# Loads of the state space issued by ScalarE, weight sums made beside the sparse attention's projections, another order in the last feed-forward

## The reference, cut to what matters

```python
att = dsa_attention(q_lat, c_kv, q_idx, k_idx, w_idx, rel_bias)   # top 128 keys by an index score
y   = ssd_scan(xh, dt, a, bm, cm)                                 # 4 groups x 4 chunks of 128 tokens
x   = x + (sigmoid(g_att) * y_att + sigmoid(g_ssm) * y_ssm) @ w_out
u   = causal_depthwise_conv(rmsnorm(x) @ w_ffn_up, conv_w, conv_b)   # 3 taps, 2 x 2816 channels
gate, val = split(u)
x   = x + (silu(gate) * val) @ w_ffn_down
```

## Time and profile before

| | |
|---|---|
| median of 3 runs | 2824.82 us (2823.62 to 2826.15) |
| the profiled execution | 2823.57 us, of which span 2821.8 us |
| TensorE matmuls busy | 95% of the span |
| VectorE, ScalarE, GpSimd busy | 60%, 46%, 7% |
| mean granted TensorE clock | 0.987 |
| HBM read, written | 439.29 MB, 159.51 MB |

### The profile page before, as it was taken

How to read it: one execution, slowest core, us unless ns; L and a number is a source line. 1 busy time by engine, 2 the same in 40 slices (tenths; PEclk the granted TensorE clock), 3 DMA queues, 4 the chain that set the end, 5 groups by cost and what they waited for, 6 DMA issues and landing times.

```text
span 2821.8 us, 43044 instructions
## 1 busy us (share of the span) xinstructions
PE 2683.9 (95%) x16783; PEld 2283.3 (81%) x16783; DVE 1681.2 (60%) x2880; ACT 1285.4 (46%) x2071; POOL 199.6 (7%) x253
## 2 busy tenths in 40 slices
PE   7999999999999999999999999889977999999997
PEld 6877889999889789689898777657756777798996
DVE  3444486264655455585374428763767975686774
ACT  3456455153535335364262534443443453465551
POOL 1110100001000000000000010330111110000000
PEclk9999999999999999999999999999998999999999
DMA  9984836858475464837352234203699792254441
GB/s 352 205 194 102 202 90 226 207 172 247 109 220 167 132 172 143 237 101 207 108 183 93 74 109 155 78 31 130 206 234 222 216 206 105 82 165 150 149 165 52
DMA packets 173724, 451.52 MB, mean 160 GB/s; under 512 B 15064, under 2 KB 15064, under 8 KB 172896
## 3 DMA queue, kind: packets, MB, share of 16 engines
q1 hardware_dynamic: 108656, 265.34, 27.7%
q0 software_dynamic: 62432, 176.17, 26.7%
q10 hardware_dynamic: 2448, 7.41, 0.7%
HBM read 439.29 MB, written 159.51 MB: 212 GB/s over the span
## 4 chain that ended last, share of the span: by engine, by line
PE 76%; DVE 9%; ACT 5%; issue 5%; DMA 4%; POOL 0%; ACTq 0%; DVEq 0%; POOLq 0%
PE ps L405 26%; PE ps L1505 22%; PE ps L554 5%; PE ps L3248 4%; PE ps L2285 2%; PE ps L1942 2%; DMA weight_sums<-in_weights 2%; PE ps L912 2%; DVE w_lo L376 2%; DMA steps_abc<-acum_rows 2%; PE ps L2087 2%; PE ps L1969 2%; PE ps L791 2%; PE ps L2814 1%; ACT w_hi L368 1%
## 5 line engine op out<-in xcount | busy, mean ns | idle before, releaser
L376 DVE TENSOR_TENSOR w_lo<-raw,w_hi 128x1024 fp32r<-128x1024 f32 x502 | 613.7, 1223 | 502.5 <-ACT w_hi L368 501.6
L368 ACT ACTIVATE w_hi<-raw 128x1024 fp32r<-128x1024 f32 x502 | 528.1, 1054 | 508.5 <-PE ps L405 301.3
L1505 PE MATMUL ps<-x_hi,w_hi 128*128 128x264 f32 (+1 forms) x1120 | 319.4, 285 | 9.6 <-DVE f_in L3398 7.8
L1505 PE MATMUL ps<-x_hi,w_lo 128*128 128x264 f32 (+1 forms) x1120 | 317.6, 284 | 0.0
L1505 PE MATMUL ps<-x_lo,w_hi 128*128 128x264 f32 (+1 forms) x1120 | 317.3, 283 | 0.0
L405 PE MATMUL ps<-x_hi,w_hi 128*128 128x512 f32 (+1 forms) x704 | 257.4, 382 | 36.4 <-DVE w_lo L376 17.3
L405 PE MATMUL ps<-x_lo,w_hi 128*128 128x512 f32 (+1 forms) x704 | 253.1, 376 | 0.0
L405 PE MATMUL ps<-x_hi,w_lo 128*128 128x512 f32 (+1 forms) x704 | 251.8, 375 | 0.0
L1505 PEld LDWEIGHTS ps<-x_hi,w_hi 128*128 128x128 f32 x1120 | 212.1, 189 | 15.6 <-DVE f_in L3398 7.5
L1505 PEld LDWEIGHTS ps<-x_lo,w_hi 128*128 128x128 f32 x1120 | 212.3, 190 | 0.5
L1505 PEld LDWEIGHTS ps<-x_hi,w_lo 128*128 128x128 f32 x1120 | 212.6, 190 | 0.0
(11 more groups left out here) (489 smaller groups left out, 5926.9 us busy)
## 6 DMA issues: line engine op xcount, KB each, us to landing
raw<-in_weights SPq DMA_DIRECT2D x257, 512.0 KB
raw<-weight_sums SPq DMA_DIRECT2D x280, 256.0 KB
weight_sums<-in_weights POOLq DMA_DIRECT2D x36, 1536.0 KB, 19.4
raw<-in_weights SPq DMA_DIRECT2D x210, 256.0 KB
weight_sums<-in_weights POOLq DMA_DIRECT2D x12, 2048.0 KB, 31.2
weight_sums<-in_weights POOLq DMA_DIRECT2D x12, 1792.0 KB, 18.9
weight_sums<-weight_sums POOLq DMA_DIRECT2D x12, 1536.0 KB, 14.3
weight_sums<-weight_sums POOLq DMA_DIRECT2D x4, 2048.0 KB, 20.3
```

The source lines that it names most:

```text
L368: nc.scalar.activation(w_hi[:, s], raw[:, s], ACT.Copy).then_inc(hi_ready, 1)
L376: nc.vector.tensor_tensor(w_lo[:, s], raw[:, s], w_hi[:, s], ALU.subtract).then_inc(lo_ready, 1)
L1505: last = nc.tensor.matmul(out_, w[:, s, 4 * (b % 2) + k], a, start=kind in "125" and k == n == 0, stop=k == 3 and n == 2, skip_group_check ...
```

## The change

It has three parts. The loads of `steps_abc` go from GpSimd to ScalarE: loads 0 and 1 after the second item of the first inputs, load n + 1 when chunk n begins. The first two groups of weight sums go into `dsa_loads`, behind the first four bias loads and ahead of the wait for `selected`; the copies of the third go to the end of `dsa_loads`, its three sums to `ssm_loads`. In the feed-forward the gate inputs have three buffers in place of two (`x_sum` is the third), the convolutions and what follows are put at later blocks (for the last two tiles at earlier ones), ScalarE splits the next chunk ahead of the pieces where no down chunk is at that block, and the down chunk at block 130 goes behind the last block.

```diff
-MIXED = {"sevenf": (54, 58, 64, 68, 74, 78, 84, 90, 98, 104, 110, 116, 122, 130, 140, 142)}
+MIXED = {"sevenf": (54, 58, 64, 68, 74, 78, 84, 90, 98, 104, 110, 116, 122, 140, 142, 144)}
...
             for h in range(4):
                 near_load(h)
+            for group in (FFN_SUMS, FFN_SUMS + 1):
+                for part in SUM_PARTS:
+                    part(pool, group)
             pool.wait_ge(selected, 1)
...
             pool.dma_start(gate[:].rearrange("p k n -> p (k n)"), gate_dram).then_inc(gate_in, 16)
+            sums_copy(pool, FFN_SUMS + 2)
...
+        def steps_load(eng, n):
+            g, c = divmod(n, CH)
+            src = bass.AP(tensor=acum_dram.tensor, offset=8 * g * SEQ + c * P, ap=[[0, P], [SEQ, 8], [1, P]])
+            eng.dma_start(steps_abc[:, n % 2], src).then_inc(abc_in[n % 2], 16)
...
             pool.wait_ge(acum_out, 16)
-            for n in range(SSM_GROUPS * CH):
-                g, c = divmod(n, CH)
-                if n >= 2:
-                    pool.wait_ge(abc_used, n - 1)
-                src = bass.AP(tensor=acum_dram.tensor, offset=8 * g * SEQ + c * P, ap=[[0, P], [SEQ, 8], [1, P]])
-                pool.dma_start(steps_abc[:, n % 2], src).then_inc(abc_in[n % 2], 16)
-                for step in ((2 * n, 2 * n + 1) if n < 6 else (n + 6,)):
-                    if step < len(SUM_STEPS):
-                        sums_step(pool, step)
-                if c == 2 and g in (1, 2):
+            for part in SUM_PARTS[1:]:
+                part(pool, FFN_SUMS + 2)
+            for g in range(1, SSM_GROUPS):
+                if g < SSM_GROUPS - 1:
                     pool.wait_ge(u_norm, 4 * g)
                     kept_back(pool, z_buf, 4 * (g - 1), z_in)
-                if c == 2 and g == SSM_GROUPS - 1:
+                else:
                     pool.wait_ge(u_lo_s, 4 * g)
                     kept_back(pool, gates, 8, gates_in)
...
-            for item in FIRST_ITEMS[0:6]:
+            for i, item in enumerate(FIRST_ITEMS[0:6]):
                 item_split(act, item, split_hi)
                 item_act(act, item)
+                if i == 1:
+                    act.wait_ge(acum_out, 16)
+                    for n in range(2):
+                        steps_load(act, n)
...
                     act.wait_ge(dec_args, n + 1)
+                    if 1 <= n < SSM_GROUPS * CH - 1:
+                        act.wait_ge(abc_used, n)
+                        steps_load(act, n + 1)
...
+                self.gate_in = [self.f_in[:, 0], self.f_in[:, 2], x_sum[:, 0:SEQ + 4]]
...
-                    at_ = dict(tap_v=b4 + 1, conv_v=b4 + 2, tap_g=b3 + 1, conv_g=b3 + 2, silu=b3 + 4, prod=b3 + 5, hi=b3 + 6, lo=b3 + 7)
+                    at_ = dict(tap_v=b4 + 1, conv_v=b4 + 3, tap_g=b3 + 2, conv_g=b3 + 4, silu=b3 + 6, prod=b3 + 7, hi=b3 + 8, lo=b3 + 9)
                     if i == SEVEN["sevenf"] - 2:
-                        at_.update(silu=b3 + 3, prod=b3 + 4, hi=b3 + 4, lo=b3 + 5)
+                        at_.update(conv_v=b4 + 2, tap_g=b3 + 1, conv_g=b3 + 2, silu=b3 + 3, prod=b3 + 3, hi=b3 + 4, lo=b3 + 4)
                     if i == SEVEN["sevenf"] - 1:
-                        at_.update(tap_v=b3 + 2, tap_g=b3 + 2, conv_v=b3 + 3, conv_g=b3 + 3, silu=b3 + 4, prod=b3 + 4, hi=b3 + 5, lo=b3 + 5)
+                        at_.update(tap_v=b3 + 1, tap_g=b3 + 1, conv_v=b3 + 2, conv_g=b3 + 2, silu=b3 + 3, prod=b3 + 3, hi=b3 + 4, lo=b3 + 4)
...
+            def inputs_free(self, eng, f, half):
+
+                wait(eng, f_conved, 2 * (f - 2) + 1 if half else 2 * (f - 3) + 2)
...
                     for c in mixed_at(name, b):
                         split_hi(act, Step(mixed_chunk(name, c) + AHEAD))
+                    behind = mixed_at(name, b)
+                    if not behind and b % 2 == 0 and b < len(order):
+                        split_hi(act, Step(seven_chunk(name, b) + AHEAD))
                     for piece, f in self.steps.get(b, ()):
...
-                    if b % 2 == 0 and b < len(order):
+                    if behind and b < len(order):
                         split_hi(act, Step(seven_chunk(name, b) + AHEAD))
```

More of the change, by code:

```diff
@@ L348, in program @@
         FFN_SUMS = len(SUM_GROUPS) - 3
[L349 to L357, removed]
         SUM_PARTS = (sums_copy, sums_of_two, sums_of_three, sums_of_four)
@@ L3191, in slot, with inputs @@
                 return 2 * (f % 2) + half
+            def inputs(self, f, half):
+                return self.f_in[:, self.slot(f, 1)] if half else self.gate_in[f % 3]
             def part(self, i, half, tokens):
-                return self.f_in[:, self.slot(i + 2, half), 2 + self.w * tokens:2 + self.w * (tokens + 1)]
+                return self.inputs(i + 2, half)[:, 2 + self.w * tokens:2 + self.w * (tokens + 1)]
+            def inputs_free(self, eng, f, half):
+                wait(eng, f_conved, 2 * (f - 2) + 1 if half else 2 * (f - 3) + 2)
             def taps(self, f, half):
@@ L3206, in tap @@
                 slot = self.slot(f, half)
-                nc.scalar.activation(self.f_conv[:, slot], self.f_in[:, slot, 2:2 + SEQ], ACT.Identity,
+                nc.scalar.activation(self.f_conv[:, slot], self.inputs(f, half)[:, 2:2 + SEQ], ACT.Identity,
                                      scale=par[:, w(2)], bias=par[:, b]).then_inc(f_begun, 1)
@@ L3224, in conv @@
                 slot = self.slot(f, half)
-                convolve(dve, self.f_conv[:, slot], 3, w, self.f_in[:, slot], b, f_conved, begun=True)
+                convolve(dve, self.f_conv[:, slot], 3, w, self.inputs(f, half), b, f_conved, begun=True)
             def product(self, dve, f):
@@ L3240, in pool @@
                 nc.gpsimd.memset(self.f_in[:, :, 0:2], 0.0).then_inc(zeroed, 1)
+                nc.gpsimd.memset(x_sum[:, 0:2], 0.0).then_inc(zeroed, 1)
             def down_products(self, pe, g, u, rows, out_, ready=None):
@@ L3252, in mixed_out @@
             def mixed_out(self, c):
-                return tile_out(Step(FIRST_TILE["sevenf"] + c), False)[:, 0, :] if c >= 14 else ps[:, 0, 0:SEQ]
+                return tile_out(Step(FIRST_TILE["sevenf"] + c), False)[:, 0, :] if c >= 13 else ps[:, 0, 0:SEQ]
             def mixed_pe(self, pe, c):
@@ L3259, in mixed_pe @@
                     self.first_banks_free(pe, "sevenf")
-                tiles_out(pe, u if c < 15 else u - 1)
+                tiles_out(pe, u if c < 14 else u - 1)
                 rows = range(8) if c < 8 else range(8, 14)
@@ L3292, in keep @@
                     src = early_out(t, False) if t < 2 else tile_out(Step(u), False)
-                    nc.scalar.activation(self.f_in[:, t:t + 1, 2:2 + SEQ], src, ACT.Copy).then_inc(evicted[u % 2], 1)
+                    nc.scalar.activation(self.inputs(t // 2, t % 2)[:, 2:2 + SEQ].unsqueeze(1), src, ACT.Copy).then_inc(evicted[u % 2], 1)
                 def both_taps(f):
@@ L3299, in both_taps @@
                         self.tap(act, f, half)
-                act.wait_ge(zeroed, 3)
+                act.wait_ge(zeroed, 4)
                 split(0)
@@ L3322, in seven_act @@
                 order = seven_order(SEVEN[name])
-                for b in range(self.last_step + 1):
+                for b in range(max(MIXED[name]) + 3):
                     if 1 <= b <= len(order):
@@ L3333, in seven_act @@
                         elif kind == "4":
-                            act.wait_ge(f_conved, 2 * (i + 1))
+                            self.inputs_free(act, i + 2, 1)
                             nc.scalar.activation(self.part(i, 1, 0), self.out_of(name, "4", i), ACT.Copy, scale=-1.0).then_inc(seven_kept, 1)
@@ L3384, in added @@
                     nc.vector.tensor_tensor(o, o, self.mixed_out(c), ALU.add).then_inc(evicted[u % 2], 1)
[L3385 to L3388, removed]
+                for b in range(max(MIXED[name]) + 3):
+                    for c in mixed_at(name, b - 1 if b < len(order) else b - 2):
+                        added(c)
                     if 1 <= b <= len(order) and order[b - 1][0] in "273":
@@ L3393, in seven_dve @@
                         dve.wait_ge(seven_kept, kept_[kept_kind, i])
-                        dve.wait_ge(f_conved, 2 * (i + 1))
+                        self.inputs_free(dve, i + 2, int(kind == "7"))
                         dst = self.part(i, int(kind == "7"), int(kind != "2"))
@@ L3413, in seven_dve @@
                         split_lo(dve, Step(seven_chunk(name, b) + AHEAD))
-                    if b >= len(order):
-                        for c in mixed_at(name, b - 2):
-                            added(c)
         HIDDEN = 2 * 32
```

## The result

The changed kernel took 2842.05 us (median of 4, 2840.6 to 2843.82) against 2824.32 us for the kernel before (median of 4 runs, one more than in the table of the kernel before): ratio 1.0062, 95% interval 1.0045 to 1.0079, 17.7 us slower. The profiled execution has a span of 2841.9 us and a mean granted clock of 0.981.

A forecast was written before the change was run, and what follows sets the result against it. TensorE matmuls, busy 95% of the span, were taken as the bound. Terms +67 + 3 - 34 - 10 = +26 us on a 2824.82 us median gave 2851 us, range 2832 to 2872.

The forecast's parts named there:

- Delay of `combo`, +67 and +3 for the clock: Sparse attention: two groups of sums outlast the selection, delaying `combo` 67 us; the clock then starts low, 3 us.
- The first group: Sparse attention: six pairs of weight sums, from first copy to issue of the fourth sum, taken as 68 us.
- the second: Sparse attention: the sequence of sums for seven pairs, taken as 83 us; 75 by size.
- State space, -34: State space: ScalarE's loads end the late-load waits, 29.6 us, and half-clock stretches, 4.6 us; bounds 28 and 36.
- So the three waits go: State space: with ScalarE issuing `steps_abc` loads, VectorE's three waits for them, 30.9 us, disappear.
- the rule of the Trainium skill: DMAs of all issuing engines share 16 DMA engines; by it, moving the state-space loads brings next to nothing.
- Rival 2: State space: ScalarE's loads are late as well, the 34 us gain stays away, 2885 us; chance 7%.
- Third group, 0: Its copies beside `att_out` and three sums in the state space's first inputs lengthen no wait: 0 us.
- Feed-forward, -10: Last feed-forward: new order and third gate buffer recover start and tail losses, 10 us; bounds -21 and +3.
- The gap at the start: Last feed-forward, first 91 us: half of 9.1 us without matmuls returns with `conv_g` made earlier, -4 with rounding.
- the tail: Last feed-forward's end: moved down chunk covers a 5.2 us wait; with other gap and half clock, -6 of 8.3.
- The fit of the Trainium skill: GpSimd DMA takes 2.0 us plus bytes at 436 GB/s; both groups, 67 us, would fit before the selection ends.

The follow-up runs named there:

- three_groups: Changed kernel with the third group of weight sums also ahead of the wait for `selected`: 2912.47 us in one execution.
- a_alone: Kernel before with only the `steps_abc` loads moved to ScalarE, all sums left in the state space: 2816.94 us against 2819.85, ratio 0.9986.
- b_alone: Kernel before with only the weight sums moved, third group's at chunks 2, 4 and 6, GpSimd still loading `steps_abc`: 2858.24 us against 2819.85, ratio 1.0131.
- the two pairs of kernels: Kernel before with new feed-forward, sums in second feed-forward or spread out, each with ScalarE or GpSimd loading `steps_abc`: ratios 0.9878 and 0.9895, 0.9827 and 0.9824.
- c_mixed: Kernel before with only the down chunk moved from block 130 to behind the last block: 2822.55 us against 2821.2, ratio 1.0006.
- c_order: Kernel before with the feed-forward edits except the moved down chunk: 2802.04 us against 2820.82, ratio 0.9933.
- early_sums: Kernel before with ScalarE's `steps_abc` loads, the feed-forward edits, and all three groups of sums in the second feed-forward: 2787.43 us against 2819.85, ratio 0.9878.
- early_gpsimd_loads: As early_sums, but GpSimd issues the `steps_abc` loads: 2788.59 us against 2820.82 for the kernel before, ratio 0.9895.

## Why the prediction was right or wrong

The direction and the size held: 17.7 us slower, 26 forecast, inside 2832 to 2872. Taken by terms:

- *Delay of `combo`, +67 and +3 for the clock.* Measured +74.6 up to the first `combo` and -0.8 behind it, 73.8 where I had 70. The mechanism is shown by the row after, and by three_groups, where a further group added 73.4 us. That the size came out so well is in part luck: the two terms inside were off in opposite directions. The first group took 84.5 us to its fourth sum, not 68, above my bound of 69.9; the second took 74.1 from its first copy, not 83, below the 75 that I had by size. In the first group the step of two sums took 35.3 us against 22.3 in the earlier trace rows. I had taken the 0.39 share of other traffic into account with a few us only. In that step it is nearly half of the work, since ScalarE's stores (q10, the gate's 2 MB among them) fall in it beside the weights (q1); in the step of the earlier trace rows the weights were the only other traffic, with 12.1%. This is the likely reason for the longer step, not one that was tested by itself. Queue, packets, MB and share of the 16 engines from 1731 to 1767 us:

```profile
q0 software_dynamic: 1568, 3.15, 52.4%
q1 hardware_dynamic: 878, 3.20, 24.9%
q10 hardware_dynamic: 854, 3.39, 23.7%
```

  The second group had nothing beside it from 1788 to 1863 us, where q0 alone moved data, as I had written.
- *State space, -34.* Measured -34.1, and that the two agree is luck, for this is the step that failed: "So the three waits go" was said of part A. a_alone gained 5.2 us in that stage, b_alone 37.1. I had seen that the loads were issued late and land late (27.7 us in the earlier trace rows), and priced only the first. Two things were missing: the loads met the sums themselves on the DMA engines, and the load of `z_buf` stayed in GpSimd's program behind those sums. Part B ended both. ScalarE's issues themselves took 0.37 us each, 6 us in all, within my bounds. My argument that the rule of the Trainium skill ("DMA: Bandwidth & Descriptors", Issuing engines are not separate DMA queues) doesn't speak to this wait was right for a part of it only: the waits at `c_row` and `c_dec` did shrink by 22 us. But by that rule A alone brings next to nothing, and a_alone brought 3 or 4 us; the two pairs of kernels, where no sum is waited for in front of a load that counts, agree with it too. Rival 2 describes what happens in a_alone, where the sums are still there; in the changed kernel two groups had been taken away, and that is why its time did not come.
- *Third group, 0.* One load was waited for 3.1 us beside its sums (until 2124.24 us); the one that took 35.9 us was of the two issued at 2054.64 us, and nothing waited for it. The stage is 3.0 us longer than in b_alone, where these came later; that is no more than the stage varies by itself, so 0 stands.
- *Feed-forward, -10.* Measured -18.2, inside my bound of -21. The gap at the start went from 9.1 to 2.4 us and the clock of the stretch from 0.96 to 1.00; the tail went from 6.3 to 0.35 us of 30. The term was too small by 8 us. The larger part, 13.9 us, is ScalarE's split ahead of the pieces, an edit that I had listed under the change and not priced; I had read the waits at `f_in` as VectorE's convolutions standing ahead of the sum. And the moved chunk, to which I had given the tail's 5.2 us, is worth nothing (c_mixed; and c_order, without it, has the whole gain of the stage).
- *The fit of the Trainium skill* ("DMA: Bandwidth & Descriptors", Anatomy of one DMA), by which both groups would have fitted before the selection: the trace disagrees as the prediction said; four copies of 1.5 MB took 29.3 us (1702.05 to 1731.31) and one sum 19.9 (1766.62 to 1786.51), where an estimate by it gives about 16 and 6.

Whether the -1.4 us ahead of the bias loads is of the change stays open; nothing was edited there, and the same point lies between 1698.6 and 1703.1 us in the kernels whose earlier part is unchanged.

## What to carry to other kernels

A right sum can rest on a wrong cause: where a change has parts, run each alone before one is kept for its gain; here one part alone was worth 3 or 4 us and another carried both the 34 us gain and the 74 us loss. A chain of transfers whose issuing program waits between steps must not stand ahead of a wait that others hang on; lay its steps at points where the previous one has long landed. And a transfer that is late has two causes, issued late and served late; moving the issue to another engine only helps with the first, and only for the loads that are moved: look for the next one that stands behind the same wait.

## What the runs showed of the hardware

A load of 512 KB in 512-byte pieces, issued by ScalarE, landed in 5.3 us in the median in the changed kernel, but in 16.7 (up to 32.3) beside copies and sums on GpSimd's queue (a_alone): another queue does not shield it. In the kernel before, on GpSimd's own queue beside the same sums, it was 13.4 (up to 27.7).

Copies and sums in HBM took so much of the DMA engines (share 0.97 with the weight stream, 0.37 without) that a stream which by itself kept TensorE busy for 270 of 274 us starved it by some 20 us over three groups (bias loads at 1725.23 us in early_sums and 1719.62 in early_gpsimd_loads, 1698.6 to 1703.1 in the others).
